# The opening of a two-layer diffusion trunk: order of its loads, a fourth place for modulation weights, tables in two groups, work moved between engines

## The reference, cut to what matters

```python
def rmsnorm(x, g):
    xf = x.astype(jnp.float32)
    xf = xf * lax.rsqrt(jnp.mean(xf * xf, axis=-1, keepdims=True) + EPS)
    return (xf * g.astype(jnp.float32)).astype(x.dtype)

mod = silu(c) @ p['w_mod'] + p['b_mod']            # c_ctx for the context tokens
shift, scale, gate = jnp.split(mod, 3, axis=-1)
h = rmsnorm(x, p['g_pre']) * (1.0 + scale) + shift
proj = h @ p['w_in']                               # 1024 x (4 mixers)
pa = proj[..., :N_A]                               # mixer A: q, k, v, z and 16 columns "ab"
...
# four mixers (A: gated delta rule, B: long convolution, C: neighbourhood attention,
# D: differential attention), merged by sigmoid gates, projected by w_out
x = x + gate * rmsnorm(y, p['g_post'])
```

## Time and profile before

| | us |
|---|---|
| median of 3 runs | 2570.09 (2566.98 to 2571.42) |
| profiled execution, its own time | 2568.52 |
| its span | 2566.9 |
| mean granted TensorE clock | 0.993 of full |
| PE busy | 2460.8 (96% of the span) |
| DVE busy / ACT busy / POOL busy | 1331.9 / 986.3 / 320.6 |
| first PE instruction of the opening | starts at 16.35 |
| first instruction of the fold of the ab rows | starts at 57.25 |

### The profile page before, as it was taken

How to read it: one execution, slowest core, us unless ns; L and a number is a source line. 1 busy time by engine, 2 the same in 40 slices (tenths; PEclk the granted TensorE clock), 3 DMA queues, 4 the chain that set the end, 5 groups by cost and what they waited for, 6 DMA issues and landing times. The chain is left out here.

```text
span 2566.9 us, 56396 instructions
## 1 busy us (share of the span) xinstructions
PE 2460.8 (96%) x23200; PEld 2336.1 (91%) x23200; DVE 1331.9 (52%) x2342; ACT 986.3 (38%) x1870; POOL 320.6 (12%) x398
## 2 busy tenths in 40 slices
PE   6999989999999999999989998999999999999998
PEld 5889889999999999879988888899999999988898
DVE  4566652677433434653555666427773343356534
ACT  3545532333234424442355455323332353254422
POOL 1222210000011101100012222100000010011000
PEclk9999999999999999999989999999999999999999
DMA  7101014111244323214221110231113332222132
GB/s 266 44 31 39 31 40 141 44 42 50 100 110 98 86 100 96 69 50 145 83 82 37 39 38 23 82 109 42 45 50 91 87 93 81 85 65 72 40 112 83
DMA packets 55687, 193.88 MB, mean 76 GB/s; under 512 B 9032, under 2 KB 9198, under 8 KB 55328
## 3 DMA queue, kind: packets, MB, share of 16 engines
q1 hardware_dynamic: 40304, 147.34, 17.1%
q0 software_dynamic: 15152, 43.24, 6.3%
HBM read 177.97 MB, written 8.39 MB: 73 GB/s over the span
## 5 line engine op out<-in xcount | busy, mean ns | idle before, releaser
L716 PE MATMUL proj<-h_hi,w_hi 128*128 128x320 f32 x3072 | 748.5, 324 | 10.5 <-DVE h_lo L2099 7.0
L716 PE MATMUL proj<-h_lo,w_hi 128*128 128x320 f32 x3072 | 705.8, 310 | 0.0
L716 PE MATMUL proj<-h_hi,w_lo 128*128 128x320 f32 x3072 | 699.5, 309 | 1.2 <-issue 1.2
L2099 DVE TENSOR_TENSOR w_lo<-raw,w_hi 128x1024 fp32r<-128x1024 f32 x232 | 288.9, 1245 | 517.5 <-ACT w_hi L1549 517.3
L716 PEld LDWEIGHTS proj<-h_hi,w_hi 128*128 128x128 f32 x3072 | 504.6, 189 | 31.3 <-issue 8.9
L716 PEld LDWEIGHTS proj<-h_lo,w_hi 128*128 128x128 f32 x3072 | 517.5, 189 | 0.0
L716 PEld LDWEIGHTS proj<-h_hi,w_lo 128*128 128x128 f32 x3072 | 514.5, 188 | 0.0
L716 PE MATMUL mix<-area 64*64 64x64 f32 (+7 forms) x8176 | 475.6, 238 | 27.4 <-DVE area L2308 11.7
L716 PEld LDWEIGHTS mix<-area 64*64 64x64 f32 (+4 forms) x8176 | 403.1, 142 | 87.5 <-issue 44.7
L1549 ACT ACTIVATE w_hi<-raw 128x1024 fp32r<-128x1024 f32 x232 | 245.7, 1059 | 584.3 <-PE proj L716 397.1
L1549 ACT ACTIVATE area<-mix 128x384 f32<-128x384 f32 (+8 forms) x422 | 187.0, 466 | 566.9 <-PE mix L716 416.8
(11 more groups left out here) (294 smaller groups left out, 2682.0 us busy)
## 6 DMA issues: line engine op xcount, KB each, us to landing
raw<-in_w_in SPq DMA_DIRECT2D x128, 512.0 KB, 3.5
raw<-in_w_mb SPq DMA_DIRECT2D x96, 512.0 KB, 3.5
raw<-in_w_mod POOLq DMA_DIRECT2D x32, 512.0 KB, 4.6
area<-in_bias POOLq DMA_DIRECT2D x64, 128.0 KB, 4.5
raw<-in_w_out SPq DMA_DIRECT2D x16, 512.0 KB, 3.5
merged<-in_w_mod SPq DMA_DIRECT2D x10, 512.0 KB, 7.2
out_x<-area SPq DMA_DIRECT2D x10, 512.0 KB, 2.6
area<-in_x_sample SPq DMA_DIRECT2D x2, 2048.0 KB, 8.6
```

The costliest lines, as they stand in the source:

```text
L716: return T.matmul(out, l, r, start=start, stop=stop)
L2099: return V.tensor_tensor(out, a_, b_, op)
```

## The change

It touches only layer 0's opening.

- SP: pairs 0 and 1 are issued ahead of the input; the input goes in five transfers of one tile each, with one semaphore for tiles 0 and 1 and one for tiles 2 to 4; there are four places for pairs (the fourth, `pair_area`, in `area`), so pairs 0 to 3 are issued without a wait and pair p waits for the products of pair p-4.
- POOL: three tables come first (condition, identity, vectors). The other five and the four of `load_small` are issued behind the power of the input's statistics. The masks `level` are issued one pair's products later.
- PE: `rows(p)` is 8 matmuls of 256 columns in place of 16 of 128. `channels(1)` stands ahead of `rows(2)`. The ab products are cut in three: slices 0 to 4 stand between piece(5) and piece(6), slices 5 and 6 between piece(6) and piece(7), slice 7 behind piece(7).
- ACT: `rows(0)` and `rows(1)` are copied ahead of the squares; ACT multiplies tiles 3 and 4 of the input, DVE tiles 0 to 2.
- DVE: the work on the small tables (`tables`, `ab_weights`, `lam_products`) moves from the start to behind h_split(0), ahead of shift_and_scale(3).

```diff
-MOD_RING = 4
+MOD_RING, MOD_SLOTS = 4, 4
...
-        mod_slots = [raw[:, RING:2 * RING], view(merged_t, 2, KT, 128), view(merged_t, 2, KT, 128, at=2 * D)]
+        mod_slots = [raw[:, RING:2 * RING], view(merged_t, 2, KT, 128), view(merged_t, 2, KT, 128, at=2 * D), pair_area]
...
-        N_CONST = 8 * 16
+        N_FIRST, N_REST = 3 * 16, 5 * 16
...
+            def load_x_tiles():
+                for t in range(TILES):
+                    src = I["x_sample"][128 * t:128 * t + 128, :] if t < 4 else I["x_prompt"]
+                    here = x_early if t < 2 else x_late
+                    sp.dma_start(x_tm[:, t, :], src).then_inc(here.sem, here.step)
...
-            load_x()
...
                 if layer == 0:
                     load_pair(0)
                     load_pair(1)
+                    load_x_tiles()
                     load(0, I["w_in"][0, 0, 0, :, :])
-                    load_pair(2)
+                    for p in range(2, MOD_SLOTS):
+                        load_pair(p)
...
-            for dst, src in ((cond_raw, I["cond"]), (vecs_t, I["vecs"]), (ident, I["ident"]), (ones, I["ones"]), (tri_t, I["tri"]),
-                             (strict_t, I["strict"]), (dist, I["dist"]), (small_t, I["small"])):
-                pool.dma_start(dst[:, :], src).then_inc(consts_in.sem, 16)
+            for dst, src in ((cond_raw, I["cond"]), (ident, I["ident"]), (vecs_t, I["vecs"])):
+                pool.dma_start(dst[:, :], src).then_inc(consts_first.sem, 16)
...
                 if layer == 0:
+                    power(layer, x_sq, 1, x_rn, 5)
+                    for dst, src in ((dist, I["dist"]), (tri_t, I["tri"]), (ones, I["ones"]), (strict_t, I["strict"]), (small_t, I["small"])):
+                        pool.dma_start(dst[:, :], src).then_inc(consts_rest.sem, 16)
                     load_small(0)
-                    pool.wait_ge(consts_in.sem, N_CONST)
-                    power(layer, x_sq, 1, x_rn, 5)
+                    pool.wait_ge(consts_rest.sem, N_REST)
...
-                        mod_products(mod_slots[p % 3], [out[:, 0, x, :] for x in range(2)])
+                        for k in range(KT):
+                            g = 32 * (k % 4)
+                            last = mm(out[g:g + 32, 0], cond[:, k, :], mod_slots[p % MOD_SLOTS][:, :, k, :], k < 4, k >= 4)
+                        last.then_inc(mod_mm.sem, mod_mm.step)
...
                     piece(5)
+                    pe.wait_ge(ab_split.sem, ab_split.at(0, 1))
+                    pe.wait_ge(mod_ready.sem, mod_ready.at(0, KT))
+                    for x in range(2):
+                        ab_half(0, x, range(5))
                     piece(6)
+                    for x in range(2):
+                        ab_half(0, x, (5, 6))
                     piece(7)
-                    pe.wait_ge(ab_split.sem, ab_split.at(0, 1))
-                    ab_half(0, 0)
-                    ab_half(0, 1).then_inc(ab_mm.sem, ab_mm.step)
+                    ab_half(0, 0, (7,))
+                    ab_half(0, 1, (7,)).then_inc(ab_mm.sem, ab_mm.step)
...
                     rows(0)
                     rows(1)
+                    for t in range(TILES):
+                        if t in (0, 2):
+                            here, n = ((x_early, 2), (x_late, 3))[t // 2]
+                            act.wait_ge(here.sem, n * here.step)
+                        last = A.activation(x_n_v[:, t, :], x_tm[:, t, :], ACT.Square, accum_out=stat[:, t:t + 1])
+                    last.then_inc(x_ss.sem, x_ss.step)
+                    act.wait_ge(x_rn.sem, x_rn.at(0, 1))
+                    for t in (3, 4):
+                        last = copy(x_n_v[:, t, :], x_tm[:, t, :], stat[:, t:t + 1])
+                    last.then_inc(act_opening.sem, act_opening.step)
...
                     split_lo(0, 0, 0)
                     shift_and_scale(2)
                     h_split(0)
+                    tables()
+                    ab_weights(0)
+                    lam_products(0)
                     for k in range(3, KT):
```

More of the change, by code:

```diff
@@ L159, in program @@
         proj_taken = Signal("proj_taken", 4 * BRANCH_PROJ, first=2)
-        mod_in, later_in = ([Signal(f"{n}{i}", 0, step=16) for i in range(k)] for n, k in (("mod_in", 3), ("later_in", 2)))
+        mod_in, later_in = ([Signal(f"{n}{i}", 0, step=16) for i in range(k)] for n, k in (("mod_in", MOD_SLOTS), ("later_in", 2)))
         mod_mm, mod_row, mod_sel = (Signal(n, KT + MOD_PAIRS) for n in ("mod_mm", "mod_row", "mod_sel"))
@@ L238, in program @@
         level_in = pre.take(LEVELS * 384)
+        pair_area = pre.take(2, KT, 128)
         end = Area(TILES * D)
@@ L412, in _ @@
                     load_pair(1)
+                    load_x_tiles()
                     load(0, I["w_in"][0, 0, 0, :, :])
-                    load_pair(2)
+                    for p in range(2, MOD_SLOTS):
+                        load_pair(p)
                     start(sp)
-                    for p in range(3, KT):
+                    for p in range(MOD_SLOTS, KT):
                         load_pair(p)
@@ L504, in _ @@
                 if layer == 0:
-                    pool.wait_ge(mod_mm.sem, mod_mm.at(0, 6))
+                    pool.wait_ge(mod_mm.sem, mod_mm.at(0, 7))
                     held(pool)
-                    pool.dma_start(level_in[:, :], I["level"]).then_inc(level_here.sem, 16)
+                    pool.dma_start(level_in[:, :], I["level"]).then_inc(consts_rest.sem, 16)
                 def load_later(b, j):
@@ L776, in turn_input, with ab_half @@
                     last.then_inc(xt_mm.sem, xt_mm.step)
-                def ab_half(layer, x):
+                def ab_half(layer, x, ks=range(KT)):
                     at, of = 1024 + 512 * x, slice(HALF * x, HALF * x + HALF)
-                    for k in range(KT):
+                    for k in ks:
                         mm(M[0:32, at:at + HALF], ab_both[:, k, :], h_hi_v[:, k, of], k == 0, False)
@@ L815, in turned @@
                             pe.wait_ge(x_n.sem, x_n.at(0, 1))
+                            pe.wait_ge(act_opening.sem, 2)
                         if k >= 2:
@@ L831, in _ @@
                     channels(0)
+                    channels(1)
                     rows(2)
-                    channels(1)
                     turned(0)
@@ L1543, in _ @@
             begin(act, 1)
-            act.wait_ge(consts_in.sem, N_CONST)
+            act.wait_ge(consts_first.sem, N_FIRST)
             act.wait_ge(cond_zero.sem, 1)
-            A.activation(cond[:, :, 0:2], cond_raw[:, :].rearrange("p (k g) -> p k g", g=2), ACT.Silu).then_inc(cond_ready.sem, cond_ready.step)
+            A.activation(cond[:, :, 0:2], cond_raw[:, :].rearrange("p (k g) -> p k g", g=2), ACT.Silu).then_inc(act_opening.sem, act_opening.step)
             def copy(out, x, scale=1.0):
@@ L1587, in _ @@
                 if layer == 0:
-                    act.wait_ge(x_in.sem, x_in.at(0, 2))
-                    for t in range(TILES):
-                        last = A.activation(x_n_v[:, t, :], x_tm[:, t, :], ACT.Square, accum_out=stat[:, t:t + 1])
-                    last.then_inc(x_ss.sem, x_ss.step)
                     def turned(k):
@@ L2224, in _ @@
                     shift_and_scale(0)
+                    shift_and_scale(1)
+                    dve.wait_ge(x_ss.sem, x_ss.at(layer, 1))
+                    V.tensor_scalar(stat[:, 0:5], stat[:, 0:5], 1.0 / D, EPS, ALU.mult, ALU.add).then_inc(x_sq.sem, x_sq.step)
                     dve.wait_ge(x_rn.sem, x_rn.at(layer, 1))
-                    for t in range(TILES):
+                    for t in range(3):
                         last = V.tensor_scalar(x_n_v[:, t, :], x_tm[:, t, :], stat[:, t:t + 1], None, ALU.mult)
                     last.then_inc(x_n.sem, x_n.step)
-                    shift_and_scale(1)
                     split_lo(0, 0, 0)
@@ L2820, in _ @@
                 fence()
-                dve.wait_ge(x_in.sem, x_in.at(layer, 1 if layer else 4))
+                dve.wait_ge(x_in.sem, x_in.at(layer, 1 if layer else 2))
                 if layer:
```

42 lines of the change are left out of this document (20 added, 22 removed).

## The result

| | before | changed |
|---|---|---|
| median of 9 runs, us | 2569.82 | 2577.08 |
| lowest to highest | 2566.66 to 2572.63 | 2574.02 to 2582.53 |
| profiled execution, us | 2568.52 | 2578.6 |
| its span; mean granted clock | 2566.9; 0.993 | 2577.0; 0.989 |

The time ratio is 1.0034, with a 95% interval of 1.0025 to 1.0044: the change makes the kernel slower by 6.4 to 11.3 us. The two medians themselves lie 7.3 us apart. Forecast were 2577.9 us and a range of 2572 to 2582.

A forecast was written before the change was run, and what follows sets the result against it. PE, working 96% of the span, was taken as the bound, with DVE and ACT chains holding it. Terms 2.7 + 1.3 + 0 + 2.8 + 1.0 = +7.8 us gave a median of 2577.9, range 2572 to 2582.

The forecast's parts named there:

- the two causes: Opening: tables land late and hold rows(5), +2.7 us; tail runs late from piece(5) to fold, +2.8; chance 0.60.
- start: Up to h_split(0): waiting for three tables instead of eight makes the start earlier, worth 1.4 us.
- tables: rows(5): DVE waits for late-issued tables, then works on them ahead of shift_and_scale(3); rows(5) at 35.3 instead of 32.60, +2.7 us.
- clock behind it: PE at half clock after idling: +1.3 us after the wait at rows(5), +1.0 after the wait before the fold.
- wide products: rows steps: half as many matmuls, twice as wide, cost the same because time goes per column; 0, at best -1.4 us.
- tail: piece(5) to fold: Early ab products delay piece(7), and DVE's ab copy stands behind the convolution; 13.0 us instead of 10.2, +2.8.
- sum at 78.9 us: All terms of the opening added, expected to carry as one shift to the end: +7.8 us, ends +1.8 and +10.2.
- the clock rule of the earlier trace: After PE idled 1.73 us, its granted clock was 0.50, the 1.2 GHz level, for the next 3 us.
- rival 3: rows steps cost per matmul, so wide products halve them; sum -0.4 us, 2569.7; chance 0.07 with anything else faster.
- Rival 1: Late tables arrive in time or nearly so at rows(5); sum about +4 us, 2574; chance 0.20.
- Rival 4: The tail does not cost, as if the ab copy were not behind the convolution; +4.0 us, 2574; chance 0.03.
- Rival 2: DVE's three multiplications block POOL's table issues, landings 2.0 us later; rows(5) +4.7, sum +9.8, 2579.9; chance 0.10.

The follow-up runs named there:

- e1: Changed kernel with all ab products back behind piece(7); 2572.38 us, ratio 1.0018 against the kernel before.
- e2: Changed kernel with DVE's small-table work, ab weights and lambda products moved behind h_split(3); 2572.64 us, ratio 1.0025 against the kernel before.
- e3: Changed kernel with ab products back behind piece(7) and DVE's table work behind h_split(3); 2567.78 us, ratio 1.0002 against the kernel before.
- e10: Changed kernel, ab products behind piece(7), table work behind h_split(3), unneeded identity products in four PE idle times; 2563.49 us, ratio 0.9988 against the kernel before.
- e4: Changed kernel plus unneeded identity products on PE, 10 ahead of rows(5) and 14 ahead of the fold; 2568.38 us, ratio 1.0005 against the kernel before.
- e9: Changed kernel with ACT multiplying all five input tiles and DVE none; one execution, 2576.61 us beside 2567.44 for the kernel before.
- e5: Changed kernel with DVE's layer-0 copy of the ab rows ahead of the convolution and masks; 2575.36 us, ratio 1.0026 against the kernel before.

## Why the prediction was right, term by term

The forecast 2577.9 and the measured 2577.08 agree, and so do the two causes; e1, e2 and e3 show them one by one. That the numbers agree to within 1 us is in part luck, as the second row shows. The terms, by the trace and then by the runs that isolate them:

| term | forecast | trace | by which run |
|---|---|---|---|
| start | -1.4, inside the next | +0.1 | e10: there at full clock, -1.4 |
| tables: rows(5) | +2.7 | +2.78 | e2: 2.30 of it |
| clock behind it | +1.3 | +1.37 | e4: 1.41 |
| wide products | 0 | 0 | 1.07 for 1.08 a step |
| tail: piece(5) to fold | +2.8 | +2.71 | e1: 2.67 |
| clock behind it | +1.0 | +1.54 | e1 and e4: 1.53 |
| sum at 78.9 us | +7.8 | +8.40 | e3 leaves 1.34 |

*Two errors cancelled in the second row.* The start's gain did not come: I had worked out the start with PE at full speed, and did not price that PE with 3 to 4 us of idle time ahead of turned(0) turns at the low clock. I applied the clock rule of the earlier trace rows to the idle times that the change adds at rows(5) and at the fold, but not to those of the start. Against that, DVE's wait was shorter than forecast: 1.46 us of waiting, because DVE came 1.5 later and the ab weights landed in 6.1 us, close to the 6.5 taken. The work was 2.00. PE's idle time was 2.60 and not 4.8, since its own products up to piece(0) had slid to 32.8 as well. The clock fell all the same, so that term held.

*Two readings behind the clock terms.* The slow step of 1.93 us that the prediction cites stands at 16.35, where the column reads 1.00, so these rows don't show that the length follows the clock. In the same trace rows(2) shows it, 1.93 in a stretch at 0.50:

```profile
23.62 1.93 PE L716 MATMUL mix<-merged,cond 128*32 128x128 f32 x32 [2.94 <-DMA merged<-in_w_mod]
```

```profile
24.00:26.00 2.00, 2.00 (x35) 1.51 (x28) 0.74 (x2) 0.00 (x0) 0.64 (x1) 0.50 1.02 408
```

And the high end of a clock term, half of 3.4 us and 1.7 "at most", rests on no row: the earlier trace rows show 3 us. In the start of the changed kernel the clock was low for 10 us, in e2 for 6.5, and there 2.66 us were lost behind the fold.

*What held by its mechanism.* The wide products cost what the narrow ones did: 16 of them 1.07 at the full clock, 32 before 1.08. That ends rival 3. Rival 1 had DVE hardly waiting; waits were short indeed, but the work and the late start put rows(5) at the forecast place, so it did not come. Rival 4 is excluded by e1 against the changed kernel. Rival 2 is real in kind, at a third of its price: ab_w was issued at 27.30 for a forecast 26.4, of which 0.6 is DVE's (e9) and the rest the later power. On the rule of the Trainium skill's page "SBUF — State Buffer", section "SBUF: two separate sides": the trace agrees, one instruction at a time. DVE's 2.08 us are three multiplications, and asked for one by one they end at 23.17, 23.83 and 24.50; the three issues end at 23.29, 23.95 and 24.61, each 0.11 to 0.12 behind one of them. So an issue was held for at most the multiplication under way (0.1 to 0.4 us longer each), and not for all three, which is what the prediction priced at 2.0. The 2.0 us of the Trainium skill's page "DMA: Bandwidth & Descriptors", section "Anatomy of one DMA — SWDGE (gpsimd) path", does not hold here: the late tables landed in 5.3 to 7.0 us, whatever their size (2.5 KB in 5.4, 128 KB in 5.4). Behind the opening of the kernel before, groups of 64 KB transfers by POOL took 1.9 to 2.8 us (medians), nearer to it.

*What stays open.* How much of the ratio beyond the opening belongs to the change: between 79 and 1600 us the distance moved by 0.6 us at most, and at the end by about 1 more, in a single execution. Each of e1 and e2 is told apart from the changed kernel by its trace; the intervals of their ratios overlap with its own. And how the fills gain more than the opening shows stays open.

## What to carry to other kernels

Work moved to a later place is priced by who stands behind it on its engine, and work moved earlier by whether its consumer can take it: here small table work went ahead of the scale that PE needs next (+2.8), and early products stood idle until a copy that is behind a convolution (+2.7). Every idle time of TensorE that such a move makes or merely shifts is then to be priced twice, once as waiting and once as the low clock behind it (here about half of the wait on top), at all places and not only at the new ones. Where idle time can't be taken away, a few unneeded products in it are a cheap trial: they were worth 0.13% in the kernel before and 0.29% in the changed one, where the whole rebuilt opening was worth nothing that the medians tell. Most of that gain arose behind the filled places, by a way that no run here shows, so it has to be tried and can't be worked out.

## What the runs showed of the hardware that I had not expected

- Filling PE's idle times pays although it adds work: 22 unneeded products of 128 columns took the kernel before from 2567.44 to 2563.46 us, ratio 0.9987 [0.9978, 0.9996]. Only 0.6 us of it is gained in the opening.
- The granted clock does not follow one idle time alone: it fell behind 2.60 and 3.57 us (changed kernel), and to 0.50 behind idle times of 1.56 (e3), but stayed at 1.00 behind 2.03 (e5) and, in e4, behind the idle time of 1.74 where before it had fallen after 1.73.
- In the start the clock column can read 1.00 while steps have the low clock's length: rows(0) 1.93 us in the kernel before, and rows(2), turned(0) and rows(3) 1.94, 1.30 and 1.94 in e5.
- POOL's issue of a transfer ended 0.11 to 0.12 us behind the end of the DVE multiplication beside it, three times in a row (changed kernel).
- A small table's landing hardly depends on its size while the 16 engines are full (share 1.00 to 1.07, 311 to 426 GB/s, 22 to 34 us in the changed kernel): 5.3 to 7.0 us for 2.5 to 128 KB.
- fp32 products on 32 columns of weights cost by columns streamed: 16 of 256 columns 1.07 us, 32 of 128 columns 1.08, and both 1.93 at the 1.2 GHz level (23.62 in the kernel before, 35.38 in the changed one).
